# Forward-substitution rows in one run and two GpSimd products on VectorE, in the RWKV stage of a hybrid layer

## The reference

```python
    log_w = -DECAY_SCALE * jax.nn.sigmoid(w0 + jnp.tanh(wd) @ w2)
    a = jax.nn.sigmoid(a0 + ad @ a2)
    kk = (k * k_k).reshape(B, S, RWKV_HEADS, HEAD_DIM)
    kk = kk / jnp.maximum(jnp.linalg.norm(kk, axis=-1, keepdims=True), 1e-12)
    k = k * (1.0 + (a - 1.0) * k_a)
    ...
    def step(state, inp):
        r_t, w_t, k_t, v_t, kk_t, a_t = inp
        sa = jnp.einsum('bhij,bhj->bhi', state, -kk_t)
        state = (state * w_t[:, :, None, :]
                 + sa[..., :, None] * (kk_t * a_t)[:, :, None, :]
                 + v_t[..., :, None] * k_t[:, :, None, :])
        return state, jnp.einsum('bhij,bhj->bhi', state, r_t)
```

## Time and profile before

| | us |
|---|---|
| three executions | 3973.13, 4002.47, 3957.53 |
| median | 3973.13 |
| the profiled execution | 3973.13 |
| its span, first to last instruction | 3971.2 |
| `recur`, its thirteen inner steps | 498.43 |

### The profile page before, as it was taken

The page is one execution under the profiler, slowest core; times in us unless marked ns, Lnnn a source line. Parts: engine busy times, 40 slices in busy tenths (PEclk is TensorE's granted clock), DMA queues, the critical chain, the costliest instruction groups (busy, mean ns, idle before and its releaser), DMA issues. The chain is left out here.

```text
span 3971.2 us, 78617 instructions
## 1 busy us (share of the span) xinstructions
PE 3568.5 (90%) x26303; PEld 2160.9 (54%) x26303; DVE 2460.0 (62%) x4152; ACT 1797.2 (45%) x2997; POOL 1502.7 (38%) x1508
## 2 busy tenths in 40 slices
PE   6699999999999982999999489989989989997999
PEld 4344444444444432888888355555555555554444
DVE  6434153241433426766874299999999999994554
ACT  2323232232322323545552256766766666773333
POOL 1001011010100103556664257767767767771222
PEclk7799999999999995868885599999999999998999
DMA  7111211112111122212210110111101101014555
GB/s 287 56 54 67 65 51 63 55 65 64 51 62 54 68 90 50 52 42 50 60 46 24 53 51 10 51 26 33 54 11 49 44 17 51 22 36 166 190 186 179
DMA packets 212461, 268.58 MB, mean 68 GB/s; under 512 B 118650, under 2 KB 164386, under 8 KB 205634
## 3 DMA queue, kind: packets, MB, share of 16 engines
q1 hardware_dynamic: 210329, 262.89, 20.7%
q0 software_dynamic: 704, 0.68, 0.1%
q10 hardware_dynamic: 1040, 0.00, 0.0%
HBM read 166.61 MB, written 96.89 MB: 66 GB/s over the span
## 5 line engine op out<-in xcount | busy, mean ns | idle before, releaser
L1882 POOL TENSOR_TENSOR plo<-p 128x512 f16<-128x512 f32 (+2 forms) x864 | 911.4, 1071 | 426.6 <-ACT p L1904 415.3
L1904 ACT ACTIVATE p<-psc,xb,sc 128x512 f32<-128x512 f32 (+3 forms) x1152 | 855.3, 743 | 440.3 <-PE psc L1995 428.6
L2047 DVE TENSOR_REDUCE mx<-pm 128x1 f32<-128x512 f32 (+3 forms) x1200 | 732.5, 636 | 75.1 <-PE pm L1926 62.3
L1974 PE MATMUL po<-v,p 128*128 128x129 f16 x4224 | 522.5, 221 | 45.6 <-ACT oev L1896 36.4
L1976 PE MATMUL po<-v,plo 128*128 128x65 f16 x4224 | 491.0, 193 | 0.0
L1974 PEld LDWEIGHTS po<-v,p 128*128 128x128 bf16 x4224 | 391.7, 98 | 150.2 <-POOL plo L1882 42.4
L623 POOL CAST stage<-qn 128x512 f16<-128x512 f32 x64 | 39.1, 610 | 1132.3 <-DVE qn L560 1132.3
L1926 PE MATMUL pm<-ka,qa 128*128 128x512 f16 (+3 forms) x1200 | 442.5, 372 | 20.0 <-DVE mx L2047 17.3
L1976 PEld LDWEIGHTS po<-v,plo 128*128 128x128 f16 x4224 | 381.5, 98 | 99.6 <-issue 1.1
L1993 PE MATMUL psc<-qa,ka 128*128 128x512 f16 (+3 forms) x1152 | 421.2, 366 | 0.0
L1995 PE MATMUL psc<-qb,kb 128*128 128x512 f16 (+3 forms) x1152 | 420.1, 365 | 0.0
(11 more groups left out here) (336 smaller groups left out, 6250.1 us busy)
## 6 DMA issues: line engine op xcount, KB each, us to landing
xt<-in_x SPq DMA_DIRECT2D x36, 512.0 KB
scratch_z<-stage SPq DMA_DIRECT2D x72, 256.0 KB, 2.0
y<-scratch_y SPq DMA_DIRECT2D x35, 512.0 KB
g<-scratch_g SPq DMA_DIRECT2D x35, 512.0 KB
xr<-in_x SPq DMA_DIRECT2D x34, 512.0 KB, 5.9
scratch_qk<-stage SPq DMA_DIRECT2D x64, 256.0 KB, 2.6
scratch_g<-stage SPq DMA_DIRECT2D x64, 256.0 KB, 2.0
out<-o SPq DMA_DIRECT2D x32, 512.0 KB, 3.0
```

The lines of the kernel that those rows point to most:

```text
L1882: nc.gpsimd.tensor_tensor(plo[:, k % NP, 0:w], p32[:, k % NP, 0:w], hi[:, 0:w], ALU.subtract)\
L1904: nc.scalar.activation(p32[:, k % NP, 0:w], psc[k % 2][:, 0:w], ACT.Exp, bias=xb[:, u, b, x // 4:x // 4 + 1], scale=m.sc[:, 0:1]).then_inc ...
L1974: nc.tensor.matmul(o[:, oc:oc + VW], hi[:, c0:c0 + P], v[:, u, x, 0:VW], start=(x == 0 and t % 2 == 0), stop=False, skip_group_check=True)
L2047: nc.vector.tensor_reduce(mx[:, s, t, q:q + 1], pm[g][:, 0, 0:w], AX.X, ALU.max).then_inc(pm_d.sem, 1)
```

## The change

Six things, all in `recur`. The forward rows 1 to 7 run without a break, ahead of `widened(n + 1, 1, ·)`. `k_new` (k times its factor, in place in `ka`) goes from GpSimd to VectorE, behind `kk_unit`. The product for `kt` goes from GpSimd's `r_k` to VectorE's `operands`, and the counter `kt_d` goes, its waits with it. `bt` and `kt` have two slots in place of three, so that `operands(b)` waits for `turn(b - 2, ·)`. `ksq` gets a buffer of its own beside `kk`, so that `kk_squares` waits for `kk_mm` alone, and `kk_unit` waits for `ar_d`. `yp` has two buffers with a semaphore each. The diff, cut to its core:

```diff
-        kk = ksq = sb("kk", [P, 2, W])
+        kk = sb("kk", [P, 2, W])
+        ksq = sb("ksq", [P, 2, W])
-        bt, kt = sb("bt", [P, 3, 2, W]), sb("kt", [P, 3, 2, W])
+        bt, kt = sb("bt", [P, 2, 2, W]), sb("kt", [P, 2, 2, W])
-        yp = sb("yp", [P, CB, 2 * P])
+        yp = sb("yp", [P, 2, CB, 2 * P])
...
-                def k_new(b):
-                    past(pool, ka_d, b, 1)
-                    done(kn_d, b, 1, tt(ka[:], zf[:, b % 2, 2:4, :], ka[:], ALU.mult))
-
                 def r_k(b):
+                    past(pool, kn_d, b, 1)
                     past(pool, tr_mm, b - 2, CB)
                     tt(rk[:, b % 2, :, :], zf[:, b % 2, 0:2, :], ka[:], ALU.mult).then_inc(rk_d.sem, 1)
-                    tt(kt[:, b % 3, :, :].rearrange("p k (c t) -> p (k c) t", t=C), ka[:].rearrange("p k (c t) -> p (k c) t", t=C),
-                       ei[:, :, 1:C + 1], ALU.mult).then_inc(kt_d.sem, 1)
...
                     if there(n + 3):
-                        k_new(n + 3)
                         a_and_r(n + 3)
...
                 def kk_squares(b):
-                    past(act, ar_d, b - 1, 2)
-                    past(act, av_d, b - 1, 1)
+                    past(act, kk_mm, b - 1, 1)
...
                 def k_factor(b):
                     past(act, gates_d, b, 1)
-                    past(act, kt_d, b - 1, 1)
+                    past(act, rk_d, b - 1, 1)
...
                 def pool_out(b):
                     past(act, pp_mm, b, 1)
-                    if b >= 1:
-                        act.wait_ge(yp_out, 16 * b)
+                    if b >= 2:
+                        act.wait_ge(yp_out[b % 2], 16 * (b // 2))
...
                 def k_scores(b, c):
-                    past(pe, kt_d, b, 1)
...
                 def kk_unit(b):
                     past(dve, kinv_d, b, 1)
+                    past(dve, ar_d, b - 1, 2)
...
+                def k_new(b):
+                    past(dve, ka_d, b, 1)
+                    tt(ka[:], zf[:, b % 2, 2:4, :], ka[:], ALU.mult).then_inc(kn_d.sem, 1)
+
                 def operands(b):
                     past(dve, av_d, b, 1)
+                    past(dve, kn_d, b, 1)
                     past(dve, exp_d, b, 1)
-                    past(dve, tr_mm, b - 3, CB)
-                    tt(chunked(bt[:, b % 3, :, :]), chunked(av[:]), ei[:, :, 1:C + 1], ALU.mult).then_inc(ops_d.sem, 1)
+                    past(dve, tr_mm, b - 2, CB)
+                    tt(chunked(bt[:, b % 2, :, :]), chunked(av[:]), ei[:, :, 1:C + 1], ALU.mult)
+                    tt(chunked(kt[:, b % 2, :, :]), chunked(ka[:]), ei[:, :, 1:C + 1], ALU.mult).then_inc(ops_d.sem, 1)
...
                     if there(n + 2):
-                        forward_rows(n + 2, 1, 4)
+                        forward_rows(n + 2)
                     if there(n + 1):
                         widened(n + 1, 1, 0)
                         widened(n + 1, 1, 1)
                         masked(n + 1, 1, akr[:, (n + 1) % 2], k_mm, k_d)
                     if there(n + 2):
-                        forward_rows(n + 2, 5, 7)
                         forward_corner(n + 2)
                     if there(n + 3):
                         kk_unit(n + 3)
+                        k_new(n + 3)
                     if 1 <= n + 1 < BLOCKS:
                         state_passed(n + 1, 0)
```

More of the change, by code:

```diff
@@ L859, in recur @@
         factor_set, zeros, pw_set = sem("factor_set"), sem("zeros"), sem("pw_set")
-        z_in, v_in, y_out = ([sem(f"{n}{s}") for s in range(2)] for n in ("z_in", "v_in", "y_out"))
-        p_in, yp_out = sem("p_in"), sem("yp_out")
+        z_in, v_in, y_out, yp_out = ([sem(f"{n}{s}") for s in range(2)] for n in ("z_in", "v_in", "y_out", "yp_out"))
+        p_in = sem("p_in")
         tanh_d, ksq_d, wa_mm, kk_mm, gates_d, ka_d, kss_d, sum_d, lc_d, kln_d, kinv_d, exp_d = (count(n, 1) for n in (
             "tanh_d", "ksq_d", "wa_mm", "kk_mm", "gates_d", "ka_d", "kss_d", "sum_d", "lc_d", "kln_d", "kinv_d", "exp_d"))
-        kk_d, av_d, kn_d, ops_d, kt_d, rk_d, f_d = (count(n, 1) for n in ("kk_d", "av_d", "kn_d", "ops_d", "kt_d", "rk_d", "f_d"))
+        kk_d, av_d, kn_d, ops_d, rk_d, f_d = (count(n, 1) for n in ("kk_d", "av_d", "kn_d", "ops_d", "rk_d", "f_d"))
         ar_d = count("ar_d", 2)
@@ L984, in _ @@
                         past(sp, pp_d, n + 1, 1)
-                        store(n + 1, pool, yp[:], yp_out)
+                        store(n + 1, pool, yp[:, (n + 1) % 2, :, :], yp_out[(n + 1) % 2])
                     if 2 <= n + 2 < BLOCKS:
@@ L997, in _ @@
                     sp.wait_ge(y_out[s], 16 * (BLOCKS // 2))
-                sp.wait_ge(yp_out, 16 * BLOCKS)
+                    sp.wait_ge(yp_out[s], 16 * (BLOCKS // 2))
             @block.gpsimd
@@ L1216, in pool_out @@
                     past(act, pp_mm, b, 1)
-                    if b >= 1:
-                        act.wait_ge(yp_out, 16 * b)
-                    activate(yp[:].rearrange("p c f -> p (c f)"), bank[3], ACT.Copy).then_inc(pp_d.sem, 1)
+                    if b >= 2:
+                        act.wait_ge(yp_out[b % 2], 16 * (b // 2))
+                    activate(yp[:, b % 2, :, :].rearrange("p c f -> p (c f)"), bank[3], ACT.Copy).then_inc(pp_d.sem, 1)
                 def r1_out(n, c):
@@ L1307, in scores @@
                             hs = rows(h)
-                            g = mm(bank[2 * c + h][:, k * 2 * C:(k + 1) * 2 * C], src[hs, b % 3, k, c * C:(c + 1) * C],
+                            g = mm(bank[2 * c + h][:, k * 2 * C:(k + 1) * 2 * C], src[hs, b % 2, k, c * C:(c + 1) * C],
                                    ar[hs, b % 4, k, c, :, :].rearrange("p j t -> p (j t)"), start=True, stop=True)
@@ L1336, in turn @@
                             nc.tensor.transpose(bank[2 * c][:, (2 * j + k) * P:(2 * j + k + 1) * P],
-                                                src[:, b % 3, k, t0:t0 + C], m.ident[:])
+                                                src[:, b % 2, k, t0:t0 + C], m.ident[:])
                     past(pe, rk_d, b, 1)
@@ L1539, in sub, with forward_rows @@
                     return f[:, o:o + 2 * (P + 8)].rearrange("p (a x) -> p a x", a=2)
-                def forward_rows(b, first, last):
+                def forward_rows(b):
                     past(dve, a_in, b, 16)
@@ L1545, in forward_rows @@
                     x8 = sub(dX, 0)[:, :, 0:P].rearrange("p a (k j) -> p a j k", j=DB)
-                    for i in range(first, last + 1):
+                    for i in range(1, 8):
                         row = sub(dA, i)[:, :, 0:DB * i:DB].unsqueeze(2).to_broadcast([DN * Q, 2, i, i])
```

## The result

| | us |
|---|---|
| before, 20 executions, median (lowest to highest) | 3962.74 (3932.7 to 4002.47) |
| after, 20 executions, median (lowest to highest) | 4006.7 (3987.35 to 4036.68) |
| ratio, 95% interval | 1.012 (1.0091 to 1.0149) |
| span of the profiled execution, before and after | 3971.2 and 4004.8 |
| the thirteen inner steps, before and after | 498.43 and 556.85 |

What follows compares the result with a forecast made beforehand. A ring through VectorE's widened(1) and TensorE, slowed by its clock falling after waits, bounds the inner steps; 390.6 + 144.4 - 3 + 12 = 544.0 against 498.4 adds 45.6 to 3973.1, giving 4019 us, range 3955 to 4060.

Steps and rivals of the forecast that it cites:

- 2.5 us for the rows: Rows 5 to 7 on VectorE ahead of widened(1) delay it and TensorE behind it by 2.5 us.
- 3 to 4 us in most steps: Sign in the profile after: TensorE's wait ahead of below(2) at 3 to 4 us instead of 0 to 1.2.
- the sum: Thirteen inner steps: 390.6 + 144.4 - 3 + 12 = 544.0 us against 498.4, 45.6 more.
- Nine of 43.4 us and four of 36.1: Inner steps 2, 3, 4 and 8 to 13 become 40.9 + 2.5 = 43.4 us; four others stay at 36.1.
- The 12 us for one stretch of 47.8: Allowance of 12 us for one TensorE low-clock stretch lasting 47.8 us instead of 20.5.
- 18.9 us at the low clock: TensorE's time from widened(1) to b_scores in step 10, against 12.0 at the high clock in step 7.
- in more than half of the stretch: Sign in the profile after: TensorE's clock at 0.50 for more than half of the inner steps' time.
- I give them nothing: Fill and drain steps around the thirteen inner steps were counted as changing by 0 us.
- The covers: Moved products (2.4 us) hide under VectorE's 3.80 us wait for X; operands' wait for turn hides before b_scores, costing 0.
- The cover over Zc: state_passed(n + 1, 0), queued behind k_new, comes 0.6 to 1.3 us later, hidden behind turn where TensorE is slow.
- about 0.6: Time in us of an elementwise product on VectorE when neither engine waits for the other, against 1.19 on GpSimd.
- order only: Rival, chance 0.22: clock falls no more often; 2.5 us on five steps, 1.5 on four, 18.5 us, 3991.6.

Runs made afterwards that it cites:

- b1_before_joined: The kernel before with one edit: forward rows 1 to 7 in one run ahead of widened(1); 4007.75 us, ratio 1.0133.
- a1_after_split: The changed kernel with one edit undone: rows 1 to 4 ahead of widened(1), 5 to 7 behind the akr mask; 3974.23 us, ratio 1.0022.
- e1_filled_behind: The changed kernel with five unread 128x128 matmuls ahead of output(n, 0), behind TensorE's wait and below(2); 3942.15 us, ratio 0.9943.
- c4_after_two_five: The changed kernel with rows 1 and 2 ahead of widened(1) and 3 to 7 behind the akr mask; 3927.22 us, ratio 0.9852.
- c1_after_filled: The changed kernel with twelve unread 128x128 matmuls in TensorE's pause, just ahead of below(2); 3952.84 us, ratio 0.995.
- d1_filled_elsewhere: The kernel before with five unread 128x128 matmuls ahead of pool_product, where TensorE is busy without a pause; 3917.46 us, ratio 0.9857.

## Why the prediction was right

**The place.** TensorE's wait for `widened(1)` ahead of `below(2)` was named as what grows, and joining the rows alone gives 1.0133 (b1_before_joined), leaving it out 1.0022 (a1_after_split). This step of the argument is shown.

**Its size.** 2.5 us for the rows, from bounds of 1.85 and 2.88; 2.23 measured. The wait was to be "3 to 4 us in most steps"; it is 3.00 in steps 2 to 12. It grew by less than the sum had it: from 1.23 to 3.00, by 1.8 and not 2.5.

**How many steps, how long.** Nine of 43.4 us and four of 36.1 were predicted; it is ten of 44.4, one of 40.7, one of 40.2 and one of 31.8. Steps 6 and 7 were kept short in the sum, because VectorE's own wait for TensorE was to absorb the rows there; they are long like the others, and VectorE has no such wait in them (1830.46 in step 6). The 12 us for one stretch of 47.8 did not come; the one longer stretch, 37.5 us, runs into step 13, the one of 40.2. The long steps are 1.0 longer than the sum: with a longer pause the clock falls at its end (1831.60 and 1831.8), where before it fell about 3 us into the work behind it (1979.04 and 1982.1 in step 10), and the low stretch is 23.9 in place of 20.5 us. The prediction's 18.9 us at the low clock counted from the second wait (1980.17), and 1.9 of them were at the high clock. A low clock "in more than half of the stretch" was to show it; it is half, 0.75 on average. So the inner steps grew by 58.4 us, not 45.6.

**The work around the inner steps.** "I give them nothing" was wrong, and it hid the miss above. Step 14 took 48.1 us before, at a clock of 0.50 all through, and 29.0 after at 0.81; with a smaller gain in the first steps, the profiled spans differ by 33.6 us, 24.8 less than the inner steps do. This is the clock again, and it varies from one execution to the next (the mean over a whole execution of the kernel before from 0.917 to 0.943, beside e1_filled_behind); the medians differ by 44.0. That the forecast of +45.6 lies so near them is partly luck of terms that cancel.

**The covers.** All held in the changed kernel. `k_new` and `kt`, 1.67 and 1.76 us beside GpSimd, 3.4 where 2.4 for both was taken, lie under waits. The cover over Zc holds where TensorE is slow, as the prediction said: in c4_after_two_five, where the clock is mostly high, TensorE waits up to 2.47 us for Zc behind `k_new`. The "about 0.6" for such a product that waits for nobody has 0.69 as its nearest row (`bt`, 1849.62). L1557's successor takes 1.00 us, and the corner begins 3.47 us behind `widened(1)`. `operands` is ready 1.27 us before `b_scores`; 1.4 was the sum's. The rule on the read interface that VectorE and GpSimd share (the Trainium skill, SBUF — State Buffer, "Who interferes with whom") fits: `bt` 0.69 and then `kt` 1.76 with GpSimd's `rk` beside them.

**The clock.** The prediction took the low stretches for an effect of the pauses, from five cases. e1_filled_behind shows that this was half of the cause: the same argument gave steps of 45 to 48 us for it, and they are 37.5, because the work behind the pause was another. c1_after_filled shows that the clock falls behind waits of 0.45 us as well. The rival "order only" (3991.6, a ratio of 1.005) is ruled out by the result itself, whose interval begins at 1.0091, and by the clock, which it left as it was: long low stretches begin in eleven steps in place of six. With the clock restored (0.95 for the inner steps) and the pause and the order left in, e1_filled_behind has 478.7 us of inner steps in place of 556.9, and that with 2.50 us more work in a step; the ratios, 1.012 and 0.9943, say some 70 us.

## What to carry to other kernels

When TensorE's clock is not at its full level in a stage, read at which instruction it falls and at which it rises before costing anything by durations: here five unread matmuls at the right place brought it back and took 78 of the 556.9 us of the stage away, while nothing hung on the longest wait of all (8.64 us). The place of work in an engine's program order matters by who waits for what is behind it; try the split at several points, since the best ones tried (two and three rows of seven) were at neither end and not where it had been put. And a control for "the pause must be filled" has to stand behind the pause, or it fills it too. Where the clock moves this much, compare medians of many executions; one profile can mislead by 20 us.

## What was not expected of the hardware

- Five 128x128 f32 matmuls that nobody reads, 1.33 us of work a step at the high clock on the busiest engine (d1_filled_elsewhere), made the kernel before 1.5% faster, in either of two places.
- A low stretch began at the end of every pause of 3.00 us (eleven of eleven), and its length went from 23.9 to 3.4 us (ten steps in either kernel) with five such matmuls behind the pause.
- With that pause filled, long low stretches still began in five steps, behind waits of 0.45 us (c1_after_filled).
- With the longer pause the steps fell into one length, 44.40 to 44.43 us ten times in a row, where those before spread from 32.9 to 52.9.
